# adaLN loads behind the residual's reload, a bias wait moved to its use, and output rows weighted between two weight splits

## The chip, the cores and the metric

The kernel runs on one core of a Trainium2 chip. The metric is the device time of one execution in microseconds (us).

## What is computed

Two trunk layers over 1024 latent tokens of width 1024. Layer 0 mixes by a 2-D DFT, layer 1 by a short gated convolution; each is followed by a grouped top-2 mixture of 16 experts. Every sub-layer is an RMSNorm with adaLN: shift, scale and gate come from `silu(c) @ w_ada[i] + b_ada[i]`.

```python
for i in range(DEPTH):                                  # DEPTH = 2
    sh1, sc1, g1, sh2, sc2, g2 = split(silu_c @ w_ada[i] + b_ada[i], 6)
    hx = rmsnorm(x, norm_mix[i]) * (1 + sc1) + sh1
    yx = fourier_mix(hx) if i == 0 else short_conv_mix(hx)
    x = x + g1 * yx
    hx = rmsnorm(x, norm_ffn[i]) * (1 + sc2) + sh2
    for e in range(N_EXPERTS):                          # comb: two non-zero weights per token
        he = silu(hx @ w_gate[e]) * (hx @ w_up[e])
        y = y + comb[:, e:e + 1] * (he @ w_down[e])
    x = x + g2 * y
```

## The kernel before

Each engine has its own instruction stream, written out by hand; streams meet only in semaphores. fp32 operands of most matmuls are split into a rounded high part and a low part, and three products are summed (high by high, high by low, low by high). ScalarE makes the high parts (WH from RAW, L922) and VectorE the low ones (WL = RAW - WH, L1455).

**Mixture of experts.** The pairs of token and expert are packed into slots of 128 rows, each slot for one expert. For slot s TensorE transposes the gathered rows, multiplies by gate and up weights (L1954), and one slot later multiplies the gated hidden values by the down weights (L1967, L1973) into PSUM banks 4 and 5. VectorE's work for one step of the loop is `body(s)`: the low part of the hidden values of slot s-1 (HETL, L1436), that of the down weights (WDL, L1440), two quarters of the weights of slot s+1 (WL), the gating of s (HE, L1444), the low part of the rows of s+1 (XTL, L1448), the first two quarters of the weights of s+2 (WL), and `y_evac(s-1)`, which multiplies the finished output rows by the router's weight and by the gate row G2 into YO (L1469). There are two YO buffers. GpSimd issues for each slot a gather of token rows (L648) and a scatter of YO that adds it into the residual in DRAM (L659). `scatter(s)` first waits for YO of s and for the landing of scatter s-1; on that landing it raises `y_added`, for which `y_evac` waits from slot 3 on. DVE reads three registers from memory (L391) at the start of every `body`. The residual of layer 0 lies in `x_dram`, that of layer 1 in `out_dram`.

**Between the layers.** When the last scatter of layer 0 has landed, GpSimd raises `moe_done`, clears the part of ACC that layer 1's remaining adaLN pieces are accumulated in (L608), and loads the bias row b_ada[1] into its first row (L610). SyncE issues the first two blocks of the convolution's input weights (WINR), then two adaLN blocks WA (`load_ada_pair(2, 0)`, 1 MB each, L413), waits for `moe_done`, and reloads the residual X in eight tiles of 512 KB (L579, the line of the DMA in the loop). ScalarE splits the two WINR blocks (L993) and squares each tile of X as it lands (L734); VectorE waits for the bias row, makes the two low parts WINL (L1554), computes the reciprocal root (VAR at L1088 and what follows) and scales the tiles (XN, L1563). The third group holds the one tile 7. When all eight are scaled, TensorE transposes (L2042) and starts the convolution's input projection (L2061, L2062, L2065). While VectorE makes the tiles ready, TensorE runs 16 dummy products (L1648), which are not needed for the result.

The accumulation of adaLN blocks into ACC (`ada_pair`, L1134) comes first behind `taps(0, 0)`, with the first output of the projection.

Of the kernel before, what the change touches and what calls it, by code (L numbers as in the profile page):

```python
# [127 lines left out]
def backbone(nc, x, c, w_ada, b_ada, norm_mix, norm_ffn, fourier_w_out, conv_w_in, conv_w, conv_w_out,  # L128
# [6 lines left out]
    def sem(name):  # L135
        return top.enter_context(nc.semaphore(name))
# [183 lines left out]
    bias_in, norm_row_in = sem("bias_in"), sem("norm_row_in")  # L320
# [141 lines left out]
    def _(sp):  # L462
# [49 lines left out]
        for layer in range(2):  # L512
# [47 lines left out]
            if layer == 0:  # L560
# [5 lines left out]
                def load_ada_pair(piece, half):  # L566

                    for k in range(2):
                        sp.wait_ge(wa_used, 4 * piece + (N_ADA - ADA_MIXER + 2 * half + k - 1))
                        load_ada(sp, 1, piece, 2 * half + k, k)  # L570
# [1 line left out]
                load_win(0, PARTS[0], 0)  # L572
                load_win(0, PARTS[1], 1)
                sp.wait_ge(w_low, PIECES * MAX_SLOTS)
                load_ada_pair(2, 0)
                sp.wait_ge(moe_done, 1)
                sp.wait_ge(cols_mm, 2)
                for m in range(NT):
                    sp.dma_start(X[:, m, :], x_dram[0][m * P:(m + 1) * P, :]).then_inc(x_back[m], 16)  # L579
                sp.wait_ge(cin_mm, 1)  # L580
                load_win(0, PARTS[2], 0)
                for n in range(3):
# [486 lines left out]
    def _(dve):  # L1069
# [178 lines left out]
        for layer in range(2):  # L1248
# [203 lines left out]
            def weights_low(s, par, e, pieces=range(PIECES)):  # L1452
                for i in pieces:
                    dve.wait_ge(w_high, s * PIECES + (b * PIECES + i + 1))
                    V.tensor_tensor(piece_of(WL[par], i), raw_piece(e, i), piece_of(WH[par], i).bitcast(f32),  # L1455
                                    ALU.subtract).then_inc(w_low, 1)
# [7 lines left out]
            def y_evac(s, par, free=True):  # L1464

                dve.wait_ge(yd_mm, s + (b + 1))
                if free:
                    dve.wait_ge(y_added, s + (b - 1))
                V.scalar_tensor_tensor(out=YO[par][:], in0=bank(4, 2), scalar=WOF[:, ds(s, 1)], in1=G2,  # L1469
                                       op0=ALU.mult, op1=ALU.mult).then_inc(yo_ready, 1)  # L1470

            def body(s, par, free=True):
                e0, e1, e2 = expert_of(s - 1), expert_of(s + 1), expert_of(s + 2)
                het_split(s - 1)
                down_low(s - 1, e0)
                weights_low(s + 1, 1 - par, e1, (2, 3))
                gated(s, par)
                xt_low(s + 1)
                weights_low(s + 2, par, e2, (0, 1))
                y_evac(s - 1, 1 - par, free)  # L1480

            def pair_slot(i, k):
                body(2 * i + (1 + k), 1 - k)
# [50 lines left out]
            if layer == 0:  # L1534
                dve.wait_ge(cols_mm, 2)
                turned = bank(6).rearrange("p (c q) -> p q c", c=4)

                def halves(a):
                    return a.rearrange("p (j c) -> p j c", j=2)

                V.tensor_tensor(halves(AC[:, 0, :]), turned[:, 0:2 * STRIP:STRIP], halves(BA[:, 0, :]), ALU.add)
                link(V.scalar_tensor_tensor(out=halves(AC[:, 1, :]), in0=turned[:, 2 * STRIP:4 * STRIP:STRIP], scalar=1.0,
                                            in1=halves(BA[:, 1, :]), op0=ALU.add, op1=ALU.add))
                V.tensor_tensor(AC[:, 1, :], AC[:, 1, :], NM[:, 1, :], ALU.mult).then_inc(cols_ready, 1)
                dve.wait_ge(cols_ready, 1)
                dve.wait_ge(bias_in, 32)


            if layer == 0:
# [59 lines left out]

                low(2, 0)  # L1610
                taps(0, 0)
                ada_pair(0, 2, 0, False)
                low(3, 1)
                gate(0, 2, 1)
# [496 lines left out]
```

## Time and profile before

| | |
|---|---|
| median of 3 runs | 1180.27 us (1179.66 to 1181.37) |
| profiled execution, its own time | 1180.38 us |
| its span | 1178.6 us |
| TensorE matmul busy | 1097.4 us (93%) |
| VectorE busy | 821.6 us (70%) |
| ScalarE busy | 497.7 us (42%) |
| GpSimd busy | 201.3 us (17%) |
| mean granted TensorE clock | 0.973 |

TensorE is busy nearly all the time, so what counts is where it is not. The chain of waits goes back from the last instruction to what released it at each step; in the trace's times the experts of layer 0 run from about 226 to 474 us, the step between the layers from there to 504 us, the convolution to about 900 us, and the experts of layer 1 from 929 to 1159 us. The time outside the span (1.8 us) is launch and end.

### The profile page before, as it was taken

Reading aid. Unit: us, or ns where it says so; the run is one execution under the profiler, and the core shown is the slowest. Engines: PE = TensorE matmul, PEld = TensorE weight load, DVE = VectorE, ACT = ScalarE, POOL = GpSimd, SP = SyncE. Lnnn points to the kernel's source line nnn. Section 1 sums busy time; section 2 is a strip of 40 time slices with the busy share of each in tenths; the row PEclk is TensorE's granted clock in tenths of the full one; section 3 lists DMA queues with packets and bytes.
Section 4 is the critical chain, followed back from the end, with each engine's and each line's share of the span. In section 5 each row is a group of like instructions: output and inputs, shape, how many; then the busy total and the mean of one; then the engine's idle time right before and its main releaser. Section 6 shows DMA issues by size and latency. Waiting matters only on the chain.

```text
span 1178.6 us, 16659 instructions
## 1 busy us (share of the span) xinstructions
PE 1097.4 (93%) x4819; PEld 806.0 (68%) x4820; DVE 821.6 (70%) x985; ACT 497.7 (42%) x681; POOL 201.3 (17%) x139
## 2 busy tenths in 40 slices
PE   4999899899999999579999999999999999999993
PEld 2554347577777777257888888878887677767772
DVE  5896985788888988355344344453565888888884
ACT  5210214376767676431111111141223466656662
POOL 2111111123333234100000000000000123223341
PEclk9999899899999999879999999999999999999997
DMA  9869549566979981603632233313235877988742
GB/s 361 330 242 384 212 178 415 198 232 184 338 235 345 343 224 24 237 16 127 251 124 93 82 111 125 125 54 124 85 131 202 343 222 267 372 295 282 209 92 34
DMA packets 82538, 243.03 MB, mean 206 GB/s; under 512 B 10592, under 2 KB 35384, under 8 KB 73276
## 3 DMA queue, kind: packets, MB, share of 16 engines
q1 hardware_dynamic: 62436, 188.88, 42.1%
q0 software_dynamic: 18496, 48.31, 16.3%
q10 hardware_dynamic: 1560, 5.26, 1.2%
q8 instruction: 24, 0.39, 0.1%
q14 instruction: 22, 0.18, 0.0%
HBM read 220.39 MB, written 40.89 MB: 222 GB/s over the span
## 4 chain that ended last, share of the span: by engine, by line
PE 65%; DVE 11%; DMA 10%; issue 8%; ACT 2%; ACTq 2%; DVEq 1%; POOL 0%; POOLq 0%
PE PS L1954 15%; PE PS L1835 7%; PE PS L2061 7%; PE PS L2065 7%; PE PS L2062 7%; DMA out_dram<-YO,TOKI 6%; PE PS L1967 3%; DVE ACC L1134 3%; PE PS L1973 3%; PE PS L1944 3%; PE PS L1686 2%; PE PS L1648 2%; PE PS L1848 2%; DMA WAE<-in_w_ada_dram 1%; PE PS L1863 1%
## 5 line engine op out<-in xcount | busy, mean ns | idle before, releaser
L1455 DVE TENSOR_TENSOR WL<-RAW,WH 128x1024 fp32r<-128x1024 f32 x204 | 240.1, 1220 | 26.0 <-ACT WH L922 24.9
L922 ACT ACTIVATE WH<-RAW 128x1024 fp32r x196 | 196.6, 1052 | 50.2 <-issue 36.7
L1954 PE MATMUL PS<-WH,XTH 128*128 128x512 f32 x384 | 154.0, 401 | 8.9 <-DVE XTL L1448 4.7
L2061 PE MATMUL PS<-HTH,WINH 128*128 128x512 f32 x384 | 150.8, 393 | 5.7 <-DVE HTL L1568 5.4
L1954 PE MATMUL PS<-WH,XTL 128*128 128x512 f32 x384 | 150.3, 391 | 0.0
L2062 PE MATMUL PS<-HTL,WINH 128*128 128x512 f32 x384 | 149.9, 390 | 0.0
L1954 PE MATMUL PS<-WL,XTH 128*128 128x512 f32 x384 | 149.8, 390 | 0.0
L2065 PE MATMUL PS<-HTH,WINL 128*128 128x512 f32 x384 | 118.7, 390 | 0.0
L1954 PEld LDWEIGHTS PS<-WH,XTH 128*128 128x128 f32 x384 | 72.1, 188 | 27.3 <-issue 13.4
L648 POOL DMA_INDIRECT XG<-h_dram,TOKI x54 | 68.1, 1261 | 113.8 <-DVE TOKI L1405 55.1
L2061 PEld LDWEIGHTS PS<-HTH,WINH 128*128 128x128 f32 x384 | 72.3, 188 | 22.3 <-DVE HTL L1568 4.8
L1967 PE MATMUL PS<-WDR,HETF 128*128 x184 | 86.6, 593 | 0.0
L2065 PEld LDWEIGHTS PS<-HTH,WINL 128*128 128x128 f32 x384 | 72.4, 188 | 15.1
L1954 PEld LDWEIGHTS PS<-WH,XTL 128*128 128x128 f32 x384 | 72.1, 188 | 15.4
L2062 PEld LDWEIGHTS PS<-HTL,WINH 128*128 128x128 f32 x384 | 72.4, 189 | 14.8
L1954 PEld LDWEIGHTS PS<-WL,XTH 128*128 128x128 f32 x384 | 72.2, 188 | 13.7
L1554 DVE TENSOR_TENSOR WINL<-WINR,WINH 128x1024 fp32r<-128x1024 f32 x24 | 29.3, 1223 | 72.6 <-ACT WINH L993 57.4
L1134 DVE SCALAR_TENSOR_TENSOR ACC<-WA,SC,ACC 128x1024 f32<-128x1024 f32 (+1 forms) x56 | 71.8, 1282 | 11.4 <-DMA WA<-in_w_ada_dram 8.0
L659 POOL DMA_INDIRECT x_dram<-YO,TOKI x24 | 52.3, 2179 | 141.5 <-DMA x_dram<-YO,TOKI 70.6
L993 ACT ACTIVATE WINH<-WINR 128x1024 fp32r<-128x1024 f32 x24 | 25.4, 1061 | 120.9 <-DMA WINR<-in_conv_w_in_dram 115.6
L638 POOL DMA_DIRECT2D out_dram<-X x8 | 4.3, 537 | 402.7 <-DVE X L1209 402.7
L913 ACT ACTIVATE XTH<-PS 128x1024 fp32r<-128x1024 f32 x50 | 51.2, 1024 | 50.4 <-PE PS L1944 47.5
(247 smaller groups left out, 1811.4 us busy)
## 6 DMA issues: line engine op xcount, KB each, us to landing
RAW<-in_moe_w_gate_dram SPq DMA_DIRECT2D x32, 1024.0 KB
RAW<-in_moe_w_up_dram SPq DMA_DIRECT2D x32, 1024.0 KB
WDR<-in_moe_w_down_dram SPq DMA_DIRECT2D x32, 1024.0 KB
WA<-in_w_ada_dram SPq DMA_DIRECT2D x28, 1024.0 KB, 8.3
WAE<-in_w_ada_dram SPq DMA_DIRECT2D x12, 1024.0 KB, 9.7
WINR<-in_conv_w_in_dram SPq DMA_DIRECT2D x24, 512.0 KB, 3.8
SLAB<-in_w_ada_dram SPq DMA_DIRECT2D x8, 1024.0 KB, 10.5
X<-x_dram SPq DMA_DIRECT2D x16, 512.0 KB, 5.9
```

What stands on the lines that cost most here:

```text
L648: pool.indirect_dma_start(out=XG[par][:], out_offset=None, in_=h_dram[layer], in_offset=bass.IndirectOffsetOnAxis(ap=TOKI[:, s:s + 1], axi ...
L659: pool.indirect_dma_start(out=x_dram[layer], out_offset=bass.IndirectOffsetOnAxis(ap=TOKI[:, s:s + 1], axis=0), in_=YO[s % 2][:], in_offse ...
L913: nc.scalar.activation(XTH[:].rearrange("p c n -> p (c n)"), bank(0, 2), ACT.Copy).then_inc(xt_act, 1)
L922: nc.scalar.activation(piece_of(WH[par], i), raw_piece(at, i), ACT.Copy).then_inc(w_high, 1)
L1134: ins = V.scalar_tensor_tensor(out=dst, in0=WA_ALL[par][:, k, :], scalar=SC[:, at:at + 1], in1=dst, op0=ALU.mult, op1=ALU.add)
L1455: V.tensor_tensor(piece_of(WL[par], i), raw_piece(e, i), piece_of(WH[par], i).bitcast(f32), ALU.subtract).then_inc(w_low, 1)
L1835: ins = T.matmul(bank(b + h), z[m % 2][:, ch, :], w[:, ch, h * BANK:(h + 1) * BANK], start=ch == 0 and i == 0, stop=ch == NC - 1 and i == 2)
L1954: ins = T.matmul(bank(2), x[:, ch, :], w[par][:, :, ch, :], start=ch == 0 and i == 0, stop=ch == NC - 1 and i == 2)
L1967: T.matmul(bank(4 + h), HETF[:], W[:, h * BANK:(h + 1) * BANK], start=True, stop=False)
L2061: T.matmul(bank(b), WINH[par][:, ch, :], HTH[:, ch, cols], start=ch == 0, stop=False)
L2062: T.matmul(bank(b), WINH[par][:, ch, :], HTL[:, ch, cols], start=False, stop=False)
L2065: ins = T.matmul(bank(b), WINL[par][:, ch, :], HTH[:, ch, cols], start=False, stop=ch == NC - 1)
```

## The change

SyncE issues the two adaLN blocks after the eight tiles of the residual. VectorE waits for the bias row just ahead of the first accumulation into ACC and no longer ahead of the first WINL. In every `body` the output rows are weighted between the two weight quarters of slot s+2 and not behind both. The number of instructions of each engine is the same.

```diff
@@ SyncE, behind the experts of layer 0
                 load_win(0, PARTS[0], 0)
                 load_win(0, PARTS[1], 1)
                 sp.wait_ge(w_low, PIECES * MAX_SLOTS)
-                load_ada_pair(2, 0)
                 sp.wait_ge(moe_done, 1)
                 sp.wait_ge(cols_mm, 2)
                 for m in range(NT):
                     sp.dma_start(X[:, m, :], x_dram[0][m * P:(m + 1) * P, :]).then_inc(x_back[m], 16)
+                load_ada_pair(2, 0)
                 sp.wait_ge(cin_mm, 1)
                 load_win(0, PARTS[2], 0)
@@ VectorE, body(s, par, free)
                 weights_low(s + 1, 1 - par, e1, (2, 3))
                 gated(s, par)
                 xt_low(s + 1)
-                weights_low(s + 2, par, e2, (0, 1))
+                weights_low(s + 2, par, e2, (0,))
                 y_evac(s - 1, 1 - par, free)
+                weights_low(s + 2, par, e2, (1,))
@@ VectorE, between the layers
                 dve.wait_ge(cols_ready, 1)
-                dve.wait_ge(bias_in, 32)
@@ VectorE, first block of the convolution
                 taps(0, 0)
+                dve.wait_ge(bias_in, 32)
                 ada_pair(0, 2, 0, False)
```

SyncE's stream between the layers. WA_75 and WA_76 are the two adaLN blocks, X is the residual. Before:

```order
L564 DMA WINR_161<-in_conv_w_in_dram 128x8x128
L564 DMA WINR_162<-in_conv_w_in_dram 128x8x128
L413 DMA WA_75<-in_w_ada_dram 128x2x1024
L413 DMA WA_76<-in_w_ada_dram 128x2x1024
L579 DMA X<-x_dram 128x1024 x8
```

and now:

```order
L564 DMA WINR_161<-in_conv_w_in_dram 128x8x128
L564 DMA WINR_162<-in_conv_w_in_dram 128x8x128
L578 DMA X<-x_dram 128x1024 x8
L413 DMA WA_75<-in_w_ada_dram 128x2x1024
L413 DMA WA_76<-in_w_ada_dram 128x2x1024
```

The two adaLN blocks stood ahead of the wait for `moe_done` and now stand behind all eight tiles.

VectorE's stream in the loop over slots, end of one `body` and start of the next. The ISA rows are waits, TENSOR_LOAD RINGI reads a register. Before:

```order
L1448 TENSOR_TENSOR XTL<-PS,XTH 128x1024
L1455 ISA
L1455 TENSOR_TENSOR WL_105<-RAW_100,WH_103 128x2x512
L1455 ISA
L1455 TENSOR_TENSOR WL_105<-RAW_100,WH_103 128x2x512
L1469 SCALAR_TENSOR_TENSOR YO_111<-PS,WOF,ROWS 128x1024
L391 TENSOR_LOAD RINGI
```

and now:

```order
L1448 TENSOR_TENSOR XTL<-PS,XTH 128x1024
L1455 ISA
L1455 TENSOR_TENSOR WL_105<-RAW_100,WH_103 128x2x512
L1469 SCALAR_TENSOR_TENSOR YO_111<-PS,WOF,ROWS 128x1024
L1455 ISA
L1455 TENSOR_TENSOR WL_105<-RAW_100,WH_103 128x2x512
L391 TENSOR_LOAD RINGI
```

YO comes one split earlier, and one split stands between it and the register reads of the next `body`.

## Rows read from the trace of the kernel before

**Rows 1.** Chain of waits, 462 to 560 us: start us, us, what.

```profile
472.56 1.29 DVE YO L1469
...
474.74 8.14 DMA x_dram<-YO,TOKI
...
486.99 5.25 DMA ACC<-in_b_ada_dram
492.33 2.36 DVE WINL L1554 x2
...
504.50 1.98 PE PS L2042 x8
...
548.39 1.21 DVE ACC L1134
```

**Rows 2.** Timeline between the layers: start us, us, engine line op [idle before <-releaser].

```profile
476.17 0.88 SPq L413 DMA_DIRECT2D WA<-in_w_ada_dram  x2
...
483.10 3.99 SPq L579 DMA_DIRECT2D X<-x_dram  x8
...
488.39 1.06 ACT L734 ACTIVATE SQ<-X 128x1024 f32<-128x1024 f32 x1 [8.41 <-DMA X<-x_dram]
...
493.43 0.19 ACT L734 ACTIVATION_READ_ACCUMULATOR SQ<-X 128x1 f32 x1
...
494.61 0.16 DVE L1088 TENSOR_SCALAR VAR<-SS 128x4 f32<-128x4 f32 x1
```

**Rows 3.** Tile X, its reloads, first at 450 to 650 us, then at 780 to 830 us.

```profile
DMA to landing us min/median/max: 5.3/8.3/10.8
...
DMA to landing us min/median/max: 2.9/4.1/7.0
```

**Rows 4.** DMA view, 40 slices: 476.3 to 484.3 us, then 1155.6 to 1161.6 us.

```profile
GB/s 0 0 20 307 0 20 61 123 143 184 102 225 164 287 225 389 246 287 266 184 328 328 328 287 348 512 389 389 430 430 328 410 492 369 430 430 451 348 430 492
...
GB/s 0 0 0 0 410 27 0 109 55 82 109 82 109 137 218 218 191 218 191 246 164 273 137 273 137 111 1 1 0 0 0 0 0 0 0 0 0 0 0 0
```

**Rows 5.** Stretches: from:to, us, busy by engine (x instructions), PEclk, DMA share, GB/s.

```profile
494.00:504.00 10.00, 0.00 (x0) 0.00 (x0) 8.49 (x27) 4.99 (x11) 0.00 (x0) 0.61 0.19 74
504.50:512.50 8.00, 6.33 (x22) 5.32 (x23) 3.75 (x4) 2.41 (x2) 0.00 (x0) 0.50 0.00 0
...
226.00:470.00 244.00, 241.58 (x1091) 185.29 (x1092) 214.60 (x222) 169.08 (x223) 81.16 (x48) 1.00 0.75 240
929.00:1159.00 230.00, 224.74 (x1004) 170.00 (x1004) 197.46 (x204) 153.86 (x205) 71.33 (x44) 1.00 0.78 250
```

**Rows 6.** Timeline of GpSimd: three of the 46 scatters.

```profile
260.58 2.49 POOL L659 DMA_INDIRECT x_dram<-YO,TOKI  x1 [6.84 <-DVE YO L1469]
...
972.24 4.04 POOL L659 DMA_INDIRECT out_dram<-YO,TOKI  x1 [5.05 <-issue]
...
1030.71 1.58 POOL L659 DMA_INDIRECT out_dram<-YO,TOKI  x1 [8.23 <-issue]
```

**Rows 7.** Timeline of VectorE beside three of them.

```profile
260.41 1.22 DVE L1440 TENSOR_TENSOR WDL<-WDR,WDH 128x1024 fp32r<-128x1024 f32 x1
...
972.46 2.35 DVE L1455 TENSOR_TENSOR WL<-RAW,WH 128x1024 fp32r<-128x1024 f32 x2
...
1029.98 1.28 DVE L1469 SCALAR_TENSOR_TENSOR YO<-PS,WOF,ROWS 128x1024 f32<-128x1024 f32 x1 [1.13 <-POOLq L658]
1032.13 0.29 DVE L1436 TENSOR_TENSOR HETL<-PS,HETH 128x128 fp32r<-128x128 f32 x1 [0.87 <-issue]
```

**Rows 8.** Waits, 945 to 1165 us: who waited for whom: us in total, times, longest.

```profile
PE PS L1954 <- DVE XTL L1448: 3.4, 8, 0.9
...
DVE YO L1469 <- POOLq L658: 4.3, 4, 1.8
```

**Rows 9.** Timeline of VectorE, end of the last slot of layer 1.

```profile
1160.07 2.36 DVE L1455 TENSOR_TENSOR WL<-RAW,WH 128x1024 fp32r<-128x1024 f32 x2 [1.85 <-ACT WH L922]
1162.35 1.28 DVE L1469 SCALAR_TENSOR_TENSOR YO<-PS,WOF,ROWS 128x1024 f32<-128x1024 f32 x1
```

## The prediction

> **What bounds the kernel now.** I read the chain of waits first, around the two places that the change touches. Between the layers TensorE does no useful work until 504.50 us [rows 1]. The chain there is: the last output rows (YO, 472.56), their scatter with an add into DRAM (474.74, 8.14 us), clearing ACC, the bias row (landed 492.2), two splits of the convolution's weights, the norm, the transposes. The reader is to see two branches in it that end close together: the bias row lets VectorE start at 492.33, and the residual's tiles let ScalarE start at 488.39 [rows 2]. Taking the bias away alone would therefore bring little: the first root needs the squares of four tiles, which are done at 493.62, and VectorE takes it up at 494.61 [rows 2], 1.0 us later. The rest must come from the tiles, and these hang on the scatter: SyncE issues them at 483.10, 0.2 us behind its landing [rows 1, 2]. During the scatter the 2 MB of adaLN weights are moving (issued 476.17), and their tail stands in front of the first tile.
>
> In the experts I read the stretches next. TensorE is idle for 2.4 us of 244 in layer 0, and for 5.3 us of 230 in layer 1 [rows 5]. The difference is the place to look for a gain or a loss from the third edit. The table of waits names it: in layer 1 VectorE waited 4 times, 4.3 us in all, for a YO buffer to be freed by a scatter, and TensorE 3.4 us for XTL behind it [rows 8].
>
> **The step between the layers.** One split costs 1.13 us from start to start (two in 2.36 us with 0.1 us of overlap) [rows 9].
>
> 1. Last YO of layer 0. It starts behind one split instead of two, 1.13 us earlier. Its product in PSUM is ready before the first split ends, so it need not wait. The scatter starts 0.9 us behind YO's end either way, provided that the scatter before it has landed. That one is released by its own YO and moves forward too (below). I take 1.13; bounds 0.2 (it doesn't) and 1.2.
> 2. The scatter's data without the adaLN loads beside it. Where nothing else moves, the 512 KB of a scatter are through at 1159.6, 4.0 us behind the end of the issue at 1155.65 (slice 27 of 40) [rows 4]; with half a microsecond for the landing that is 4.4. The last one of layer 0 ended its issue at 476.32 and landed at 482.88, 6.6 us later [rows 1], with 300 GB/s of other traffic beside its second half [rows 4]. Gain 2.1 us; bounds 0 (the add in DRAM sets the pace) and 2.6.
> 3. So the tiles are issued at about 479.9, 3.2 us earlier. ScalarE and VectorE are ready by then: the splits of WINR and WINL and the table load are over at 480.
> 4. First tile from issue to landing: 5.3 us now; in the reload of layer 1, with no other load in front, the median of the same tiles is 4.1 [rows 3]. Gain 1.2 us; bounds 0.5 and 1.5. The later tiles follow at the queue's rate as before.
> 5. The wait for the bias gone from WINL: VectorE stands ready when the squares are done. Gain 1.0 us; it can't be more, since the squares end there.
>
> Sum 1.1 + 2.1 + 1.2 + 1.0 = 5.4 us; TensorE would start at 499.1. Bounds 2.5 and 6.3, the likelier part 4 to 6.3. What is late next is the chain itself: squares, roots and scaling of eight tiles take the 9.9 us from 494.61 to 504.50 as before. Costs at nothing: the adaLN blocks now queue behind 4 MB of tiles and land about 11 us later than they did, at some 498 us; their first use, and the bias row's, is at 548.39 [rows 1], 50 us on. In SyncE's queue they stand ahead of a wait for the first output of the projection, which can't come before the transposes, so they hold nothing up.
>
> The clock: TensorE's 16 dummy products end at 493.9 in both kernels, so it would be idle for 5 us instead of 10.6. The granted clock is 0.61 over 494 to 504, which puts its fall to the lower level some 2.2 us into the idle time, and 0.50 when the transposes run [rows 5]. I expect it to fall all the same and count nothing. If it stayed up, the first eight transposes would take 1.0 us instead of 1.98 [rows 1] and the products behind them as much less again, up to 1.8 us; a later rise costs 1 us.
>
> **The last scatter of layer 1.** The same as step 1: YO starts at 1161.2 instead of 1162.35 [rows 9], and all that follows is the scatter and the end. Gain 1.1 us; bounds 0 and 1.2.
>
> **The loops over slots.** In an ordinary slot VectorE does the same work in the same time and the scatter can start 1.13 us earlier. TensorE is the bound and gains nothing. What I found in the rows on GpSimd is that a scatter takes 1.58 us to issue at best and over 4 at worst, and that the long ones end 1.45 us behind the end of a VectorE operation that reads two SBUF tiles (WDL, WL): 260.58 + 2.49 = 263.07 against WDL's end at 261.63, and 972.24 + 4.04 = 976.28 against the end of two WL at 974.81 [rows 6, 7]. With YO one split earlier the scatter starts just when that split is over and VectorE is at HETL, which reads PSUM. So scatters that wait for YO should issue in 1.6 to 3.0 us.
>
> The one that matters is at 972.24. From there the scatters of layer 1 are back to back until about 1130, each released by the landing of the last, and the loop gets behind them. It should end its issue at WDL's end plus 1.45, at 974.0 instead of 976.28: 2.3 us for the whole run of scatters. Against that, in a slot that waits for its YO buffer, HETL follows YO by 2.15 us now [rows 7], and by 1.28 + 1.13 = 2.41 with the split between: 0.26 us in each of 4 waits, 1.0 us. TensorE gains at most what it loses to these waits. Net 2.3 - 1.0, and a little for the gathers queued behind the scatters: I take 1.5 us. Bounds: a gain of 2.9 (5.3 - 2.4, the idle time above that of layer 0), a loss of 1.5.
>
> The Trainium skill, SBUF — State Buffer, section "Who interferes with whom", says that a VectorE operation with two SBUF inputs contends with GpSimd's reads only, and infers that writing DMA descriptors is not held up by a tensor_tensor. By that rule the issue of a scatter would not care what VectorE runs, and this term would be 0.3 (the earlier start alone) and the whole 1173.6. The two ends above speak against it here.
>
> **Sum.** 5.4 + 1.1 + 1.5 = 8.0 us. The profiled execution took 1180.38 us, as good as the median of 1180.27, so 1172.4.
>
> **Rivals.**
> A. As summed: 1172.4, between 1169.5 and 1175. Chance 0.68.
> B. The scatter is not made quicker by taking the adaLN loads away, because its pace is that of the add in DRAM. For it: alone it moves about 200 GB/s, far below the 430 of plain loads [rows 4]. Against: 4.0 against 6.6 us. Step 2 falls out: 1174.5. Chance 0.11.
> C. The loops give almost nothing or cost up to 1.5 us, because the issue of a scatter does not hang on VectorE, or because the shifted scatters meet other splits: 1173.6 to 1175.5. Chance 0.11.
> D. Slower. In slots where YO waits for its buffer, the next scatter starts 0.73 us behind YO (1029.98 and 1030.71) [rows 6, 7]. The split would start at 1.19 us, 0.46 us behind the scatter's start. If a split that begins so soon behind the start still holds the scatter, it is held to the split's end, 2.41 us behind YO, and ends 1.45 later, in 3.1 us instead of 1.58. The run of scatters is what releases the next YO, so this feeds itself: 1.5 us in each of 7 scatters is 10.5 against the 6.5 of the other terms, 1184.4. The split at 972.46 began 0.22 us behind the start of its scatter and held it; 0.46 is more than that, and from where on a scatter is safe no row shows. It decides against the change from 5 such scatters on, in layer 1 between 1020 and 1115. Chance 0.08.
> The remaining 0.02 is for a case that I don't see.
>
> **Numbers.** The forecast is A, 1172.4. The range takes in A, B and C: 1168.8 (A with the clock's 1.8 and a bit of the upper bounds) to 1176.5 (B and C together). About 0.2%, 2.4 us, is what a measurement can tell from no change. Faster by more, below 1177.9: 0.90. Within: 0.04. Slower: 0.06.
>
> **What would show it.** The last scatter of layer 0 issued near 473.6 and landed near 479.7; the tiles issued at 479.9 and the first square at 484; VAR at 489.2 right behind the fourth square; the first transposes at 499.1; adaLN blocks issued after the tiles with no wait at 548; scatters that wait for YO at 1.58 us of issue for the most part, and the one near 971 well under 4 us; fewer waits of YO in layer 1 and TensorE idle for 3.5 to 4.5 us of that stretch; the last YO one split ahead of its old place. Wrong would be: a scatter that takes 6 us from its issue although nothing runs beside it (B), scatters of 3.1 us behind waiting YO rows (D), or a first tile that needs over 5 us.

## The result and the profile after

The kernel with the change took 1168.88 us (median of 4 runs, 1166.43 to 1169.37), the kernel before 1179.97 beside it: a ratio of 0.990, interval 0.988 to 0.9925, some 11 us less. Carried over to the 1180.27 of the runs before, that is 1168.7, just under the low end of the range, 1168.8. In a second comparison with three times as many runs (experiment 3, below) the same kernel gave 0.9938 (0.9916 to 0.9959), 1172.09 us; carried over to 1180.27 that is 1173.0. So the sign was right, and the forecast of 1172.4 is 3.7 us above the first comparison and 0.6 below the second. That it nearly meets the second is in part luck, since one of its terms was far too small. How far it was right by its own steps the stages tell.

| | before | after |
|---|---|---|
| profiled execution, its own time | 1180.38 us | 1166.43 us |
| its span | 1178.6 us | 1164.6 us |
| TensorE matmul busy | 1097.4 us (93%) | 1091.9 us (94%) |
| VectorE busy | 821.6 us | 821.8 us |
| GpSimd busy | 201.3 us | 189.0 us |
| mean granted TensorE clock | 0.973 | 0.980 |

VectorE does the same work. GpSimd has the same instructions and is busy for 12 us less: its scatters take less time to issue. The chain of waits of the changed kernel between the layers (start us, us, what), to be laid beside [rows 1]:

```profile
469.05 1.05 ACT WH L922
470.43 1.28 DVE YO L1469
472.61 6.63 DMA x_dram<-YO,TOKI
...
480.83 6.69 DMA X<-x_dram
487.60 1.16 ACT SQ L734 x2
...
498.70 1.98 PE PS L2043 x8
```

The same branch in the timeline (start us, us, engine line op, [idle before <-releaser]), to be laid beside [rows 2]:

```profile
479.50 4.28 SPq L578 DMA_DIRECT2D X<-x_dram  x8
483.09 1.06 ACT L734 ACTIVATE SQ<-X 128x1024 f32<-128x1024 f32 x1 [5.25 <-DMA X<-x_dram]
483.82 0.94 SPq L413 DMA_DIRECT2D WA<-in_w_ada_dram  x2
...
486.32 1.06 ACT L734 ACTIVATE SQ<-X 128x1024 f32<-128x1024 f32 x1 [0.80 <-DMA X<-x_dram]
...
488.57 0.19 ACT L734 ACTIVATION_READ_ACCUMULATOR SQ<-X 128x1 f32 x1
488.79 0.17 DVE L1088 TENSOR_SCALAR VAR<-SS 128x4 f32<-128x4 f32 x1 [10.94 <-ACT SQ L734]
```

The bias row is gone from the chain, and ScalarE's squares are what VectorE waits for: it takes up VAR 0.2 us behind the last square's start of read-out, where it was 1.2 in [rows 2]. The scatter takes 6.63 us where it took 8.14, and the first tile is squared 3.6 us behind its issue, not 5.3. TensorE starts at 498.70 instead of 504.50.

The largest step is not there, though. I cut both traces at the same instructions:

| stage (us) | before | after | difference |
|---|---|---|---|
| start to the first gate product of layer 0 | 226.64 | 224.87 | -1.8 |
| from there to the last YO of layer 0 | 245.92 | 245.55 | -0.4 |
| to the first transposes of the convolution | 31.94 | 28.28 | -3.7 |
| to the first gate product of layer 1 | 424.90 | 423.37 | -1.5 |
| to the last YO of layer 1 | 232.95 | 226.20 | -6.7 |

The experts of layer 1 gave 6.7 us, where the prediction had 1.1 for the last scatter and 1.5 for the loop. The first row belongs to a stretch that no edit touches; in the fourth the moved loads and the bias row are only used for the first time. Both differ between these two executions by the granted clock. Stretches (from:to, us, busy by engine with instructions, PEclk, DMA share, GB/s) of the kernel before:

```profile
200.00:220.00 20.00, 18.83 (x104) 10.13 (x96) 14.90 (x54) 4.49 (x5) 2.06 (x2) 0.83 0.76 303
...
905.00:920.00 15.00, 13.07 (x59) 8.15 (x57) 11.29 (x40) 3.90 (x4) 0.00 (x0) 0.77 1.01 421
```

and of the kernel after, the last line its experts of layer 1:

```profile
200.00:220.00 20.00, 17.80 (x110) 9.30 (x102) 17.26 (x60) 4.53 (x6) 2.06 (x2) 1.00 0.86 343
...
905.00:920.00 15.00, 11.78 (x56) 7.18 (x57) 13.68 (x28) 1.99 (x3) 2.10 (x2) 1.00 0.90 362
...
923.00:1146.00 223.00, 221.74 (x1002) 169.56 (x1000) 196.70 (x203) 152.98 (x205) 67.84 (x44) 1.00 0.81 257
```

The clock was at 0.83 and 0.77 in two places of the one and full in the other. All 17 traces of this case agree on what such a stretch costs, whatever their edits. Up to the first gate product they take 223.4 to 223.5 us where the clock was at the lower of its two levels (1.2 instead of 2.4 GHz) for 6.8 us in all, 226.0 to 226.9 where for 17.1, and 228.4 where for 23.9. From the transposes to layer 1 it is 423.3 to 423.5 us in nine traces (e1_rows_only and e3_bias_only among them) with 8.3 to 11.2 us at the lower level, 424.5 to 425.2 in seven (e5_rows_layer1 and e13_scatter_late among them) with 12.9 to 15.5, and 426.4 in one with 18.1. These 3.3 us of the 14 between the two profiles are therefore not the change's; experiment 3 comes back to them. In the last line TensorE is idle for 1.3 us of 223, where it was idle for 5.3 of 230 [rows 5].

What happened in layer 1 shows in GpSimd's timeline after, the third to the fifth scatter and two later ones:

```profile
964.77 1.59 POOL L659 DMA_INDIRECT out_dram<-YO,TOKI  x1 [4.94 <-issue]
974.80 1.59 POOL L659 DMA_INDIRECT out_dram<-YO,TOKI  x1 [5.40 <-DVE YO L1469]
984.67 2.33 POOL L659 DMA_INDIRECT out_dram<-YO,TOKI  x1 [5.13 <-DMA out_dram<-YO,TOKI]
...
1050.60 1.58 POOL L659 DMA_INDIRECT out_dram<-YO,TOKI  x1 [7.70 <-issue]
1061.35 1.58 POOL L659 DMA_INDIRECT out_dram<-YO,TOKI  x1 [7.82 <-issue]
```

The scatter that took 4.04 us [rows 6] takes 1.59. The one behind it is released by its YO, and not by a landing. How much sooner the data are there, the view of tile YO for the scatter at 964.77 alone tells (issue to landing, us):

```profile
DMA to landing us min/median/max: 6.4/6.4/6.4
```

and for the same scatter of the kernel before its chain of waits, from the start of the issue to the landing; behind it its timeline has the fourth scatter:

```profile
972.24 13.20 DMA out_dram<-YO,TOKI
...
986.39 1.59 POOL L659 DMA_INDIRECT out_dram<-YO,TOKI  x1 [8.76 <-DMA out_dram<-YO,TOKI]
```

So with 2.45 us less of issue the landing came 6.8 us nearer to the start, not 2.3. Who waited for whom in the experts of layer 1 after (us in total, times, longest), beside [rows 8]:

```profile
POOL out_dram L659 <- DVE YO L1469: 25.0, 5, 5.4
...
DVE YO L1469 <- POOLq L658: 2.4, 3, 1.5
...
PE PS L1955 <- DVE XTL L1448: 0.7, 2, 0.4
```

TensorE waited for XTL twice, 0.7 us in all, and not 8 times for 3.4.

### The profile page after: what moved, and what is told of

It reads as the page before. It is cut to its first block, busy times and chain, and to the rows that moved or that the text cites. A ratio compares the mean times of both kernels' runs of the same rounds, so it can differ in the third digit from the quotient of the medians.

```text
span 1164.6 us, 16659 instructions
## 1 busy us (share of the span) xinstructions
PE 1091.9 (94%) x4819; PEld 803.5 (69%) x4820; DVE 821.8 (71%) x985; ACT 496.8 (43%) x681; POOL 189.0 (16%) x139
## 4 chain that ended last, share of the span: by engine, by line
PE 72%; DVE 11%; DMA 8%; issue 4%; ACT 2%; ACTq 1%; SPq 0%; DVEq 0%; POOL 0%; POOLq 0%
PE PS L1955 20%; PE PS L1836 8%; PE PS L2062 7%; PE PS L2063 7%; PE PS L2066 7%; PE PS L1968 5%; PE PS L1974 4%; DVE ACC L1134 4%; PE PS L1945 3%; DMA out_dram<-YO,TOKI 3%; DMA WAE<-in_w_ada_dram 3%; PE PS L1687 2%; PE PS L1849 2%; PE PS L1864 1%; PE PS L1679 1%
## 5 line engine op out<-in xcount | busy, mean ns | idle before, releaser
L1455 DVE TENSOR_TENSOR WL<-RAW,WH 128x1024 fp32r<-128x1024 f32 x204 | 243.8, 1219 | 38.2 <-ACT WH L922 38.0
L1448 DVE TENSOR_TENSOR XTL<-PS,XTH 128x1024 fp32r<-128x1024 f32 x50 | 61.1, 1221 | 7.9 <-ACT XTH L913 7.4
## 6 DMA issues: line engine op xcount, KB each, us to landing
RAW<-in_moe_w_up_dram SPq DMA_DIRECT2D x32, 1024.0 KB, 11.5
```

What stands on the lines that cost most here:

```text
L1448: V.tensor_tensor(XTL[:].rearrange("p c n -> p (c n)"), bank(0, 2), XTH[:].rearrange("p c n -> p (c n)").bitcast(f32), ALU.subtract).then_ ...
```

## The experiments

Three theories were to be told apart. **H, the hold:** the issue of a scatter is held by a VectorE operation that reads two SBUF tiles; putting YO between the splits moves the scatter out of their way. **E, the early start:** it only matters that the scatter starts a split earlier. **R, the run:** from some slot on the scatters of layer 1, each released by the landing of the last, set the pace of the loop, so anything that a scatter takes longer is paid once per slot. H and E say why a scatter is done sooner, R says what that is worth. All ratios are against runs of the kernel before on the same chip, with a 95% interval.

### 1. The parts alone

Only the rows between the splits (e1_rows_only):

```diff
-                weights_low(s + 2, par, e2, (0, 1))
+                weights_low(s + 2, par, e2, (0,))
                 y_evac(s - 1, 1 - par, free)
+                weights_low(s + 2, par, e2, (1,))
```

> Only the output rows between the two splits; adaLN loads and the wait for the bias row stay as before. Theory M (the recorded chain, with the term of the loops mis-sized): the last scatter of each layer 1.1 us earlier, and 4 to 6 us from the scatters of layer 1 that start sooner: 6 to 8 us faster than before, scatters that follow their YO at once issue in 1.6 us, and YO waits for its buffer 3 times or fewer in layer 1. Theory N (the loops gave 1.5 us as forecast, and the rest of the 11 us came from the loads or is scatter between executions): 3.5 to 4 us faster.

Only the adaLN blocks behind the tiles (e2_ada_only):

```diff
-                load_ada_pair(2, 0)
                 sp.wait_ge(moe_done, 1)
...
                     sp.dma_start(X[:, m, :], x_dram[0][m * P:(m + 1) * P, :]).then_inc(x_back[m], 16)
+                load_ada_pair(2, 0)
```

> Only the adaLN blocks behind the residual's tiles. Theory M: the last scatter lands 2 us sooner and the first tile comes after 4.1 instead of 5.3 us, but the bias row is still waited for (clearing ACC 3.5 us, loading it 5.3 us, two splits 2.4 us behind the landing), which ends only 1 us behind the squares: 2 to 3 us faster. Theory N: the loads carry more than that, 5 us or more. Rival S (the scatter's pace is that of the add): 1 us or less, since then the bias chain starts where it did.

Only the bias row waited for at its use (e3_bias_only):

```diff
-                dve.wait_ge(bias_in, 32)
...
                 taps(0, 0)
+                dve.wait_ge(bias_in, 32)
```

> Only the wait for the bias row moved. The squares of four tiles end at 493.6 and set the first root whatever the bias does. All theories: 1.0 us faster, within what can be measured; VAR right behind the fourth square. More than 2 us would mean that the bias chain and not the tiles was late.

Both of these together, without the rows (e4_ada_bias):

> Both edits between the layers, output rows as before. Theory M: 2.1 + 1.2 + 1.0 = 4.3 us, of which the recorded execution with all edits showed 3.7 between the last YO and the first transposes; layer 1's loops as before, with YO waiting about 4 times. Theory N: 7 us or more.

| kernel | median us | ratio | last YO of layer 0 to transposes | layer 1 |
|---|---|---|---|---|
| e1_rows_only | 1174.06 | 0.9962 (0.9947 to 0.9978) | 32.2 | 228.6 |
| e2_ada_only | 1177.69 | 1.0005 (0.9991 to 1.0019) | 30.2 | 233.4 |
| e3_bias_only | 1178.18 | 1.0005 (0.9985 to 1.0026) | 31.3 | 232.7 |
| e4_ada_bias | 1175.22 | 0.9980 (0.9962 to 0.9999) | 28.2 | 233.2 |

Between the layers neither edit alone is worth anything that the time shows; the traces have 1.8 us for the loads and 0.7 for the bias. Together they take 3.8 us off the stage (the time of the whole kernel gives 2.4, interval 0.1 to 4.5). That is the picture of two branches that end close together. With the loads alone the first square came 3.3 us behind the issue of the tiles, but VAR still 11.5, because VectorE stood at the bias row; with the bias alone the first square came after 5.8. The rows alone take 3.6 us, and they sit in layer 1: 228.6 instead of 233.

By the time alone these runs speak for theory N of the expectations, not for M: the rows gave 3.6 us (N: 3.5 to 4, M: 6 to 8), the loads none of M's 2 to 3, the bias none of its 1.0. It is the traces that put the gain of the rows into the loop of layer 1, as M has it. One sign of M is missing too: in e1_rows_only YO waited for its buffer 4 times, 6.3 us in all, not 3 times or fewer.

### 2. Which layer, and where exactly

All edits, but the rows between the splits in layer 1 only (e5_rows_layer1), and in layer 0 only (e6_rows_layer0):

```diff
-                weights_low(s + 2, par, e2, (0,))
+                early = layer == 1
+                weights_low(s + 2, par, e2, (0,) if early else (0, 1))
                 y_evac(s - 1, 1 - par, free)
-                weights_low(s + 2, par, e2, (1,))
+                if early:
+                    weights_low(s + 2, par, e2, (1,))
```

> All edits, but the output rows come between the splits in layer 1 alone. Theory M (the gain of the third edit lies in the back-to-back scatters of layer 1): within 1.5 us of the kernel with all edits, slower by the 1.1 us of layer 0's last scatter. Rival L (both layers gain alike): 3 us slower than with all edits.

> The same with the rows between the splits in layer 0 alone. Theory M: it loses what layer 1 gave, 5 to 7 us slower than with all edits, and layer 1's scatters issue in 2 to 4 us again. Rival L: 3 us slower.

All edits, and the rows ahead of both splits (e7_rows_first):

```diff
-                weights_low(s + 2, par, e2, (0,))
                 y_evac(s - 1, 1 - par, free)
-                weights_low(s + 2, par, e2, (1,))
+                weights_low(s + 2, par, e2, (0, 1))
```

> All edits, but the output rows ahead of both splits. Two parts of the third edit are told apart: YO is earlier still (up to 1.1 us, less where the product in PSUM isn't ready, and about 2 us at the end of each layer, where the first split waits for ScalarE), but the scatter now starts while a split runs. Theory H (a running split of two SBUF tiles holds the issue of a scatter): issues of 2 to 3 us in the loops instead of 1.6, the run of scatters in layer 1 starts earlier, and the time is equal to or above that of all edits by up to 4 us but for the ends. Theory E (only the earlier start counts): issues of 1.6 us, 2 to 5 us faster than with all edits.

All edits, but the adaLN blocks between the wait for the experts' end and the tiles (e8_ada_between), so that they move beside no scatter but stand ahead of the tiles:

```diff
                 sp.wait_ge(moe_done, 1)
+                load_ada_pair(2, 0)
                 sp.wait_ge(cols_mm, 2)
...
-                load_ada_pair(2, 0)
```

> All edits, but the adaLN blocks stand behind moe_done and ahead of the tiles. It parts the two reasons for moving them. The last scatter is as quick as with all edits (6.6 us from its issue), and the tiles wait for 2 MB of adaLN weights, 5.2 us at 400 GB/s. Expected: 4.5 to 5.5 us slower than with all edits. If the scatter alone mattered: no slower.

| kernel | median us | ratio | last YO of layer 0 to transposes | layer 1 |
|---|---|---|---|---|
| e5_rows_layer1 | 1169.41 | 0.993 (0.9903 to 0.9956) | 28.0 | 227.3 |
| e6_rows_layer0 | 1173.26 | 0.9966 (0.9947 to 0.9985) | 28.8 | 233.3 |
| e7_rows_first | 1163.60 | 0.9874 (0.9842 to 0.9906) | 29.0 | 225.3 |
| e8_ada_between | 1173.35 | 0.9956 (0.9938 to 0.9974) | 33.4 | 225.7 |

The gain of the rows is in layer 1; in layer 0 it is below what these runs tell. The traces say it more clearly than the times: e6_rows_layer0 is 7.6 us slower than the first comparison of the change and 3.3 slower than the second, which would fit M or L, but its layer 1 takes 233.3 us, as with late rows (rows behind both splits).

That layer 0 gains nothing is not for want of long issues. In each of the six traces with late rows in layer 0 a scatter near 268 us is held for 4.13 us too, and before 11 scatters of that layer are released by the landing of the last. But no YO of that layer waited for a buffer. The one trace with late rows in which three did (e4_ada_bias, 3.7 us in all) has the longest layer 0 of all, 249.7 us. So in these two layers a held scatter costs where the loop catches up with it.

Loads ahead of the tiles undo the gain between the layers, and more: the step is 5.1 us longer, as expected. The timeline of e8_ada_between:

```profile
478.33 0.88 SPq L413 DMA_DIRECT2D WA<-in_w_ada_dram  x2
479.25 4.37 SPq L579 DMA_DIRECT2D X<-x_dram  x8
487.62 1.06 ACT L734 ACTIVATE SQ<-X 128x1024 f32<-128x1024 f32 x1 [10.97 <-DMA X<-x_dram]
```

Its scatter landed after 6.65 us, as with nothing beside it, and then the first tile took 8.4 us to its square, not 3.6: 2 MB ahead of it in the queues cost 4.8 us.

The rows ahead of both splits are a surprise: 0.9874, where the change has 0.9902 and, below, 0.9938. In e7_rows_first VectorE's timeline at the end of layer 0 reads

```profile
467.01 1.28 DVE L1469 SCALAR_TENSOR_TENSOR YO<-PS,WOF,ROWS 128x1024 f32<-128x1024 f32 x1 [0.92 <-PE PS L1973]
468.21 2.35 DVE L1455 TENSOR_TENSOR WL<-RAW,WH 128x1024 fp32r<-128x1024 f32 x2
469.20 1.68 POOL L659 DMA_INDIRECT x_dram<-YO,TOKI  x1 [3.61 <-DVEq L1505]
```

The last YO waits for its product (L1973), and for nothing else. In the chain of the changed kernel, above, ScalarE's WH at 469.05 stands in front of YO at 470.43: the split between is one that VectorE can't do before ScalarE has made the high part, and YO stood behind it. Layer 0 is some 3 us shorter (242.8 instead of the 245.8 of the traces with the rows between the splits). 1.7 of them are that wait: the last YO starts 0.1 us behind the end of the last down product, where it was 1.8. The rest is in the slots before. Neither H nor E foresaw this run rightly: it is faster, but the issues in layer 1 average 1.79 us, as with the rows between the splits, neither 1.6 nor 2 to 3. The scatter above starts 0.99 us behind the start of the first split, which is just before that split's end, so the issue is held for 0.1 us only and takes 1.68. For the length of an issue, what decides is not where YO stands but what runs at the moment at which the scatter starts.

### 3. The better order again, and the change again

e7_rows_first once more (e10_first_again), the changed kernel once more (e9_all_again), and e7_rows_first with 24 instead of 16 dummy products between the layers (e12_first_warm):

```diff
-                keep_running(16)
+                keep_running(24)
```

> The kernel with all three edits once more, on the chip of the next three. Expected: 9 to 12 us faster than before; layer 1 from the first gate product to the last YO in 226 to 228 us against 233.

> The rows ahead of both splits, beside all edits on one chip. If its first time was no chance: 3 to 5 us faster than all edits, of which 2 at the end of layer 0, 1 in layer 1. If it was the chip: the same time as all edits.

> The rows ahead of both splits, and 24 dummy products instead of 16 between the layers, so that TensorE is idle for about 1 us instead of 7.7 before the transposes. If the granted clock stays at the upper level there: first eight transposes in 1.0 instead of 2.0 us, 1.5 to 2 us faster than with 16. If it falls all the same: no change. If the dummies end too late: up to 1 us slower.

| kernel | median us | ratio |
|---|---|---|
| e9_all_again | 1172.09 | 0.9938 (0.9916 to 0.9959) |
| e10_first_again | 1163.65 | 0.9876 (0.9851 to 0.9901) |
| e12_first_warm | 1163.14 | 0.9861 (0.9834 to 0.9889) |

The rows ahead of both splits hold up, 0.9874 and 0.9876. By how much they beat the change does not: 3 us beside its first comparison and 7 beside its second, where 3 to 5 were expected; and the change itself gave 7.3 us (4.8 to 9.9) here, not 9 to 12. The 8 dummies more keep the clock up for the first 16 transposes, which take 1.97 us in e12_first_warm,

```profile
473.60 21.64 PE L1648 MATMUL PS<-K 128*128 128x512 f32 x46
495.55 1.97 PE L2042 MATMUL PS<-K,XN 128*128 128x128 f32 x16 [0.31 <-DVE XN L1562]
```

against 3.42 in e10_first_again:

```profile
494.08 3.42 PE L2042 MATMUL PS<-K,XN 128*128 128x128 f32 x16 [5.89 <-DVE XN L1562]
```

But the clock fell in e12_first_warm too, some 5 us later (granted 0.50 over 501 to 504 us), and the time is the same within the intervals (their traces have 424.5 and 425.1 us from the transposes to layer 1).

The twelve runs of e9_all_again lie from 1163.8 to 1175.2, four below 1169 and eight above 1171.9, with nothing between, while the four of the first comparison had all been below 1170. So the same kernel was run twice more, one execution each (e14_all_look and e15_all_look), and e4_ada_bias once for layer 1 (e16_late_look).

> All edits, one look more. On the last chip its twelve executions fell in two groups, four of 1163.8 to 1168.9 and eight of 1172.0 to 1175.2, and the recorded one was of the lower. If this one is of the upper group, its trace shows which stage is 6 us longer: the loops over slots, if the pace of the scatters and expert loads differs between executions (expected), or the step between the layers.

> All edits, the third look, for the same reason as the second: a recorded execution of the upper group would show in which stage the 6 us lie; one of the lower group adds a third value for layer 1 (226 to 227 us expected).

> Both edits between the layers, rows behind both splits, one look: layer 1 from the first gate product to the last YO in 232 to 234 us, as in the five recorded executions with late rows in layer 1.

They took 1168.98, 1175.92 and 1171.27 us. The first two are one from each group, and their stages differ by 2.3 us up to the first gate product, 1.3 in layer 0, -0.2 between the layers, 3.0 from the transposes to layer 1 and 0.7 in layer 1, 7.1 in all. Stretches of e14_all_look:

```profile
200.00:220.00 20.00, 18.38 (x118) 10.29 (x118) 17.07 (x64) 4.69 (x6) 2.07 (x2) 1.00 0.88 353
502.00:530.00 28.00, 22.64 (x120) 18.31 (x119) 15.28 (x18) 10.73 (x10) 0.00 (x0) 0.96 0.11 38
```

and of e15_all_look:

```profile
200.00:220.00 20.00, 18.82 (x106) 9.84 (x104) 14.79 (x57) 4.69 (x6) 0.63 (x1) 0.83 0.82 338
502.00:530.00 28.00, 22.91 (x106) 18.41 (x106) 15.35 (x20) 9.65 (x8) 0.00 (x0) 0.77 0.03 11
```

The two stages that carry 5.3 of the 7.1 us are those in which the clock stood at 0.83 against 1.00, and at 0.77 against 0.96. The program and its chip were the same. So how long a low clock lasts in these places differs from one execution to the next, and a median of four runs can be moved by it. It was expected that the two would differ in the loops over slots; these hold 2.0 of the 7.1. Whether the clock is all that parts the two groups of e9_all_again is not shown: their mean granted clocks overlap, 0.975 to 0.982 in the lower and 0.970 to 0.978 in the upper. For the change itself the stages are the better measure, and they repeat: over the nine traces with both edits between the layers in place and the tiles ahead of the loads (the rows anywhere but ahead of both splits) the step is 27.9 to 28.8 us, against 31.9 and 32.2 without either edit. Layer 1 took 225.7 to 228.6 us in the seven traces with the rows between the splits, mean 227.0, and 231.8 to 233.4 in the six with the rows behind them, mean 232.9. With 0.5 us in layer 0 (medians) the three stages add up to 0.5 + 3.8 + 5.9 = 10.2 us, which would be 1170.1.

### 4. Is it the run of scatters?

e16_late_look has the rows at their old place, and its third scatter of layer 1 is held as in the kernel before. GpSimd's timeline, and VectorE's beside it:

```profile
964.73 4.04 POOL L659 DMA_INDIRECT out_dram<-YO,TOKI  x1 [5.05 <-issue]
979.45 1.59 POOL L659 DMA_INDIRECT out_dram<-YO,TOKI  x1 [9.33 <-DMA out_dram<-YO,TOKI]
...
963.82 1.21 DVE L1440 TENSOR_TENSOR WDL<-WDR,WDH 128x1024 fp32r<-128x1024 f32 x1
964.95 2.35 DVE L1455 TENSOR_TENSOR WL<-RAW,WH 128x1024 fp32r<-128x1024 f32 x2
```

This is no accident of one execution. In all six traces with late rows (before, e2, e3, e4, e16, e6) the third scatter takes 4.04 or 4.05 us and the fourth starts 14.1 to 15.0 us behind it. In all seven with the rows between the splits (after, e1, e5, e8, e9, e14, e15) it takes 1.59, and the fourth starts 10.0 us behind it.

To price a scatter's delay by itself, e13_scatter_late is the changed kernel with two reads of a register ahead of each scatter of layer 1, on GpSimd, behind its waits:

```diff
                 pool.sem_inc(y_added, 1)
+            if layer:
+                for _ in range(2):
+                    slots_used(pool)
             pool.indirect_dma_start(out=x_dram[layer], ...
```

> All edits, and GpSimd reads two registers from memory ahead of each scatter of layer 1, which nothing uses: the scatter issues about 1 us later (the trace will say), VectorE and the data are as they were. It doses the suspected cause. Theory R (layer 1's time hangs on the run of scatters, each released by the last): layer 1 gets longer by 5 to 10 us, more YO rows wait for a buffer, and the gain of the third edit in layer 1 is lost. Theory P (the gain is in VectorE's own order, not in the scatters): layer 1 within 1.5 us of that with all edits.

It took 1177.49 us, ratio 0.9985 (0.9971 to 1.0000): nearly all of the gain is gone, though no work was added on TensorE or VectorE. Layer 1 took 234.6 us, 7.6 more than the mean of 227.0; theory R had 5 to 10, P at most 1.5. Its waits in layer 1, and one YO with the scatter behind it:

```profile
DVE YO L1472 <- POOLq L658: 13.8, 7, 3.3
...
1003.20 1.28 DVE L1472 SCALAR_TENSOR_TENSOR YO<-PS,WOF,ROWS 128x1024 f32<-128x1024 f32 x1 [1.86 <-POOLq L658]
...
1005.19 1.87 POOL L662 DMA_INDIRECT out_dram<-YO,TOKI  x1 [10.40 <-issue]
```

Where YO waits for its buffer, the scatter starts 1.99 us behind YO instead of 0.72 (1050.60 above against YO at 1049.88, below): 1.27 us per scatter. VectorE waited 13.8 us for buffers, not 2.4. The slots between 1010 and 1065 lose 1.2 to 2.1 us each over the unhindered period. This is R: in that stretch a scatter's length is the loop's pace. Not all of the 7.6 need come by way of YO: the gathers stand behind the scatters in GpSimd's stream, and TensorE waited 2.9 us for gathered rows, where it waited for none in the changed kernel. Nor does the run settle H against E, since a later scatter also meets other splits.

Where the loss sits, the slots tell. Between the 10th and the 13th group of transposes of the hidden values (HE, L1960) in layer 1, about 1026 to 1059 us in the kernel before, three slots take 3.4 to 3.9 us more than three unhindered ones in all six traces with late rows, and YO waits for its buffer just there. In all ten with the rows between or ahead of the splits (but e13_scatter_late) they take 0.0 more, and YO does not wait there. In e13_scatter_late, whose third scatter starts 0.8 us later and is held for 3.32, they take 4.7 more.

## Why the prediction was right, and where it was wrong

**Step 1, the last YO of layer 0, 1.1 us: right, 1.2.** Behind the end of the layer's last down product YO starts after 1.6 to 1.9 us in the eight traces with the rows between the splits in layer 0, and after 3.0 to 3.1 in five of the six with late rows. The sixth is the profile of the kernel before: its last WH came 0.9 us earlier against that product, and YO followed after 2.1. That, and what the slots before do, is why the whole layer shows less, 0.4 us in the two profiles and 0.5 in the medians (245.8 and 246.3). The late ones spread from 245.8 to 249.7, so for the loop of layer 0 nothing can be told.

**Step 2, the scatter without the loads, 2.1 us: right, 1.8.** From the start of its issue the last scatter of layer 0 landed after 8.0 to 8.4 us in the three traces with the loads beside it and 6.0 to 6.8 (mean 6.4) in the fourteen without. Rival B, that the add in DRAM sets the pace, is out. (The step's own sum is slightly off: 4.0 and half a microsecond are 4.5, not 4.4; where the traces hold the landing of such a last scatter, it comes 0.3 us behind the end of its last packet.)

**Step 4, the first tile, 1.2 us, and step 5, the bias, 1.0: 1.9 together instead of 2.2.** The first square came 3.2 to 3.6 us behind the issue, 2.1 us less (means) than the 5.0 to 5.8 with the loads; the later tiles gained less (the third square waited 0.80 us for its tile, above), so that in the nine traces of the step above VAR came 9.3 to 9.9 us behind the issue instead of 11.5. Of the stage, last YO to transposes, the prediction had 4.3 us and the traces have 3.8 (3.7 in the two profiles).

**The clock, counted at nothing: right.** TensorE stood idle for 7.25 us and the clock fell all the same, 0.64 over 494 to 504 where it was 0.61 [rows 5]. It was not 5 us, as the prediction has it, because the dummy products start earlier as well and end at 491.4, not at 493.9 in both kernels. That a later rise costs 1 us, no run shows.

**The last scatter of layer 1, 1.1 us: right, 1.3.** Behind the end of the last down product of layer 1 the last YO starts after 1.9 to 2.2 us in the seven traces with the rows between the splits and 3.3 to 3.4 in the six with late rows.

**The loops over slots, 1.5 us with 2.9 at most: this is the step that failed.** The mechanism was right: the third scatter of layer 1 issues in 1.59 us, and the two YO that waited for a buffer 58 and 69 us behind its start wait no longer. (Taken over the layer the waits of YO are a poor measure, 4.4 us in the mean with late rows and 3.4 with the rows between.) The size was not: layer 1 gave 5.9 us in the means, 1.3 of it at the end and 4.6 in the loop, up to the end of the last down product. TensorE's idle time fell to 1.3 us in the profile, not to 3.5 to 4.5. The charge of 0.26 us for each YO that still waits was right (HETL follows such a YO after 2.37 us in two of three, 2.15 before). Two other things in the step were wrong, and both make the number too small.

The first is the cap. I took what TensorE could win from its idle time, "5.3 - 2.4". Here is what a stall looks like in the timeline of the kernel before; the first pair is a slot that waited for XTL, the second one that didn't:

```profile
1078.30 0.38 PE L1960 MATMUL PS<-K,HE 128*128 128x128 f32 x2
1078.97 0.49 PE L1954 MATMUL PS<-WH,XTH 128*128 128x512 f32 x1 [0.28 <-DVE XTL L1448]
...
1088.53 0.38 PE L1960 MATMUL PS<-K,HE 128*128 128x128 f32 x2
1088.67 0.48 PE L1954 MATMUL PS<-WH,XTH 128*128 128x512 f32 x1
```

From the transposes of the hidden values to the next gate product it is 0.14 us undisturbed and 0.67 in the stall. So 0.53 us was lost, and the view shows 0.28 as idle: the rest lies inside the modelled length of the product before. Measured by the period, start to start of the HE transposes, an unhindered slot takes 9.68 us, and the slots of layer 1 above 9.75 exceed that by 8.3 us in all before (11 slots) and by 2.7 after (6 slots); 0.25 us in each of 11 stalls is most of the difference to the 5.3. In layer 0 before the excess is 2.1. By the period the cap would have been 8.3 - 2.1 = 6.2, not 2.9, and the range would have held the first comparison.

The second is what the long scatter is worth. I counted its issue, 2.3 us, "for the whole run of scatters". It landed 6.8 us sooner after its start. Against the first gate product of the layer, the third scatter starts at about the same time in both (42.8 and 42.7 us), the fourth 4.3 us earlier, the fifth 5.4, the sixth 8.5. In the kernel before, a landing releases the fourth scatter, at 986.39; in the kernel after, the first one that a landing releases is the fifth, at 984.67. Where the 4.4 us beyond the issue come from the traces leave open: the gathers and loads that the late data meet are different ones.

**Rival C** is refuted here, as far as it says that the issue of a scatter does not hang on VectorE. I set all 782 scatters of the 17 traces beside what VectorE ran. A scatter takes 1.58 us, unless an operation with two SBUF inputs (WL, WDL) is running 0.13 us behind its start; then it ends 1.45 us behind that operation's end. For 731 this is right within 0.06 us. Of the others 28 took 1.58 us although such an operation was running, all with one that had begun between 0.03 us before the scatter's start and 0.13 behind it, and 23 were held longer, for 3.1 to 4.8 us, over the next ones too. No scatter took longer than 1.60 us with none of these running 0.13 us behind its start, whatever VectorE did on PSUM (YO, HETL, HE, XTL). The Trainium skill, SBUF — State Buffer, section "Who interferes with whom", infers that descriptor writing is not held up by a tensor_tensor. Applied to this scatter that does not agree with the traces: its issue is held by one. But the scatter also takes its row numbers (TOKI) from SBUF, and whether it is that reading or the writing of descriptors that is held, no run separates.

**Rival D** rested on the question whether a split that begins 0.46 us behind the start of a scatter holds it. VectorE's timeline after, beside the scatter at 1050.60 shown above:

```profile
1049.88 1.28 DVE L1469 SCALAR_TENSOR_TENSOR YO<-PS,WOF,ROWS 128x1024 f32<-128x1024 f32 x1 [0.61 <-POOLq L658]
1051.08 1.22 DVE L1455 TENSOR_TENSOR WL<-RAW,WH 128x1024 fp32r<-128x1024 f32 x1
```

The split begins 0.48 us behind the scatter's start, and the scatter took 1.58. The same at 1061.35 and 1080.33. So D did not happen, and by the 0.13 us above it had a margin of a third of a microsecond.

**H against E.** The third scatter starts at the same time in both kernels and only its hold is gone, which is H with no part of E in it; and of the 4.6 us in the loop 3.7 (means) lie in the three slots named in experiment 4. In the loop of layer 1 a YO that is earlier still brought nothing: with the rows ahead of both splits the last down product ends 225.0 to 225.5 us behind the first gate product, with the rows between them 225.0 in the mean (223.6 to 226.5). The 1.7 us by which layer 1 is shorter in e7_rows_first are its last YO, which no longer stands behind a split. What stays open is how the other 0.9 us divides, and no run holds the third scatter alone and leaves the others as they are.

## What to carry to other kernels

Take the loss of a stalled engine from the period of its loop, not from the idle time between its records, where these overlap. A chain in which each transfer is released by the landing of the last is a resource of its own: find the slot from which the loop waits for it, and price a delay once per slot from there. One long issue early in the run can cost more than itself, as in layer 1, or nothing, as in layer 0 where no buffer was waited for. And when two branches end close together, edit both before judging either: here neither showed in the time alone, and together they took 3.8 us off their stage.

## What the hardware showed that I had not expected

**The clock makes executions of one kernel differ.** e14_all_look and e15_all_look are the same program on the same chip and 6.9 us apart; 5.3 of the 7.1 us of their stages lie in the two that hold the stretches with a granted clock of 1.00 and 0.96 in the one and 0.83 and 0.77 in the other. Two low stretches of the kernel before (200 to 220 and 905 to 920 us) are in places where TensorE is busy most of the time, 18.83 of 20 us in the first, and in some executions they are missing. That is more than many an edit is worth, and it is in a profile that one compares with another.

**A scatter's issue can be held past one VectorE operation.** The hold ends in nearly all cases with the operation that was running, though another with two SBUF inputs follows with no gap. 23 of 782 were held on, and not at random: the third scatter of layer 1 in each of the six traces with late rows there, over WDL and both WL, and the one near 268 us in each of the six with late rows in layer 0. Why these, no run shows.

**2 MB in front cost the first tile of 512 KB 4.8 us** (e8_ada_between); beside the scatter (before, e1 and e3) they had cost the tile 2.1 and the scatter 1.8.
